# Subtracting the weights' low parts on VectorE instead of GpSimd, in the first group of a hybrid decoder's second stage

## The reference

```python
proj = xn @ w_in
qkv = silu(causal_depthwise_conv(proj[..., :GDN_QKV_W], conv_w))
...
sol = triangular_solve(tmat, rhs)              # within each chunk
v_new = u_c - w_c @ s                          # scan over the chunks, state s
o_c = qd_c @ s + qk_c @ v_new
s = s * dl_c + kd_c^T @ v_new
```

## Time and profile before

| | |
|---|---|
| median of three runs | 2783.84 us (2783.05 to 2786.7) |
| profiled execution, first to last instruction | 2785.0 us |
| PE busy | 2502.1 us (90%) |
| DVE busy | 1675.2 us (60%) |
| ACT busy | 1132.9 us (41%) |
| POOL busy | 457.1 us (16%) |
| POOL `p_wlo` (L1178), 72 instructions | 106.3 us, mean 1486 ns |

### The profile page before, as it was taken

One profiled execution on the slowest core, in us unless ns is written; L12 is line 12 of the kernel. 1 busy time (PEld: TensorE's weight loads), 2 busy tenths in 40 slices (PEclk: granted clock), 3 DMA queues, 4 the chain that ended last, 5 costly groups with the idle time before them and its releaser, 6 DMA issues. The chain is left out here.

```text
span 2785.0 us, 50427 instructions
## 1 busy us (share of the span) xinstructions
PE 2502.1 (90%) x17193; PEld 2202.9 (79%) x17193; DVE 1675.2 (60%) x3904; ACT 1132.9 (41%) x3326; POOL 457.1 (16%) x345
## 2 busy tenths in 40 slices
PE   5468888799999999999999779999997899999997
PEld 4467777789999899999999648878885677777775
DVE  4357676677777777777777322333332566666764
ACT  4244454444444444444444234433332233333332
POOL 0033333310000000000000012200001232233331
PEclk8689999999999999999999689999998899999998
DMA  6664444533445543443443057743456122222221
GB/s 192 196 250 148 138 154 149 188 124 127 157 134 174 161 131 127 145 135 132 138 152 113 21 175 260 253 169 140 170 200 241 65 86 83 71 75 68 85 69 48
DMA packets 273814, 392.79 MB, mean 141 GB/s; under 512 B 79282, under 2 KB 187906, under 8 KB 273442
## 3 DMA queue, kind: packets, MB, share of 16 engines
q1 hardware_dynamic: 240066, 370.05, 39.7%
q10 hardware_dynamic: 33632, 21.26, 2.6%
HBM read 267.92 MB, written 123.31 MB: 140 GB/s over the span
## 5 line engine op out<-in xcount | busy, mean ns | idle before, releaser
L1229 PE MATMUL p_psp<-xg,p_whi 128*128 128x264 f32 x4096 | 848.5, 297 | 27.7 <-POOL p_wlo L1178 17.3
L1229 PEld LDWEIGHTS p_psp<-xg,p_whi 128*128 128x128 f32 x4096 | 661.1, 193 | 32.3 <-issue 23.0
L1229 PE MATMUL p_psp<-xg,p_wlo 128*128 128x264 f32 x2048 | 610.5, 298 | 0.0
L1229 PEld LDWEIGHTS p_psp<-xg,p_wlo 128*128 128x128 f32 x2048 | 395.0, 193 | 0.0
L981 DVE SCALAR_TENSOR_TENSOR p_acc<-p_proj,p_taps,p_acc 128x528 f32<-128x528 f32 x288 | 250.3, 869 | 4.6
L1824 PE MATMUL first_q<-first_w,p_o 128*128 128x512 f32 (+1 forms) x864 | 206.5, 399 | 18.0 <-DVE first_w L1788 18.0
L2366 PE MATMUL first_q<-first_w,p_hT 128*128 128x512 f32 x720 | 195.4, 412 | 13.2 <-DVE p_q L2252 12.9
L1824 PEld LDWEIGHTS first_q<-first_w,p_o 128*128 128x128 f32 (+1 forms) x864 | 157.1, 184 | 60.7 <-issue 15.0
L862 ACT ACTIVATE p_sig<-p_sig 128x528 f32<-128x528 f32 x128 | 82.5, 644 | 289.7 <-DVE p_sig L983 289.6
L2366 PE MATMUL p_pso<-p_wo,p_oT 128*128 128x512 f32 x768 | 192.3, 401 | 7.9 <-DVE p_oT L2278 4.2
L1824 PE MATMUL p_psz<-p_wk,p_o 128*128 128x512 f32 x768 | 181.3, 392 | 0.0
(11 more groups left out here) (263 smaller groups left out, 4665.2 us busy)
## 6 DMA issues: line engine op xcount, KB each, us to landing
p_whi<-w_dram SPq DMA_DIRECT2D x92, 512.0 KB, 4.1
p_wlo<-w_dram SPq DMA_DIRECT2D x92, 512.0 KB, 5.0
raw<-w_a_in SPq DMA_DIRECT2D x36, 512.0 KB, 6.6
w_dram<-p_whi SPq DMA_DIRECT2D x34, 512.0 KB, 4.1
w_dram<-p_wlo SPq DMA_DIRECT2D x34, 512.0 KB, 5.3
p_o<-hT_dram SPq DMA_DIRECT2D x34, 512.0 KB, 4.7
hT_dram<-p_hT SPq DMA_DIRECT2D x32, 512.0 KB, 3.3
p_hT<-hT_dram SPq DMA_DIRECT2D x30, 512.0 KB, 4.0
```

The lines of the kernel that those rows point to most:

```text
L1229: ins = nc.tensor.matmul(ps_p[half_][:, 0:HALF], (w_hi, w_lo)[i][:, f, kc * P:(kc + 1) * P], xg[:, g % 2, j, kc, half_ * HALF:(half_ + 1) ...
```

## The change

`split_low` moves from GpSimd's program to VectorE's, with the same operands, the same wait for ScalarE's high part (`hi_ready`) and the same signal when it is done (`lo_ready`). In a slot it stands behind the taps and ahead of the solve rows. The six calls of the prologue move too: VectorE does them after the constants have arrived and before it waits for the zeroed scratch. Nothing else changes.

```diff
@@ block.vector
+            def split_low(it, f, part):
+
+                cols = slice(part * D // 2, (part + 1) * D // 2)
+                dve.wait_ge(hi_ready, 2 * (NF * it + f) + (part + 1))
+                nc.vector.tensor_tensor(w_lo[:, f, cols], w_raw[:, f % 2, cols], w_hi[:, f, cols].bitcast(f32),
+                                        ALU.subtract).then_inc(lo_ready, 1)
...
                     for item, f, part in slot.taps:
                         convolve(item, f, part)
+                    for item, f, part in slot.split:
+                        split_low(item, f, part)
                     for q, i in slot.rows:
                         solve_row(q, i)
...
             dve.wait_ge(const_in, 16 * N_CONST)
+            for f in range(NF - 1):
+                for part in range(2):
+                    split_low(0, f, part)
             dve.wait_ge(zeroed, 32)
             run(dve, step)
@@ block.gpsimd
-            def split_low(it, f, part):
...
-                    for item, f, part in slot.split:
-                        split_low(item, f, part)
 
             pool.wait_ge(cleared, 1)
-            for f in range(NF - 1):
-                for part in range(2):
-                    split_low(0, f, part)
             run(pool, step)
```

## The result

The kernel after takes 2798.06 us (median of 4 runs, 2794.54 to 2801.13) against 2783.52 before: 1.0055 times [1.0041, 1.0069], slower by 14.5 us. In a second series it took 2797.18 against 2779.40, 1.0063 [1.0049, 1.0077]. The forecast was slower, 2804 us, range 2784 to 2817.

What follows compares the result with a forecast made beforehand. PE waits for VectorE, chiefly for p_r, and VectorE pays for GpSimd's work. Terms -1.2 + 2 - 2 + 18.5 + 3 = +20.3 us on the profiled 2785.0 give 2805, or 2804 us on the median; range 2784 to 2817.

Steps and rivals of the forecast that it cites:

- Price of one: One 128x512 subtraction on VectorE takes 0.62 us of queue time (0.61 to 0.69), in place of 1.5 on GpSimd.
- Slots 5 to 9: Four subtractions and a 0.7 us wait against 3.8 us of relief: -0.3 for each of seven heads, -2 us in all.
- the 0.9 that was to stay: Last 0.9 us of excess in slots 5 to 9; if it stays, that term's upper bound is +3.5 us.
- Slots 14, 15 and 21: Second subtraction delays p_X by 0.55 us; after slot 21's taps the q part's clamp comes at about 383.8 instead of 383.48.
- Slot 23: VectorE waits for ScalarE's copy, then its subtraction stands for GpSimd's SiLU: p_r 2.8 us late, 1.8 without GpSimd.
- six meetings at 2.8, turns of 59 us: Slot 23's delay after heads 1 to 7: 6 x 2.8 + 1.75 = 18.5 us; heads take 55 and 59 us.
- the turns swallow it: Rival: the new wait runs beside some 3.15 us at the loop's turns, three of six meetings cost nothing; 2788 us, 13%.
- the start costs all of it: Rival: head 0's term at 6 us and the clock's at 6; 2814 us and above, 8%.
- relief wins: Rival: VectorE's queue gains more than it gets, slot 23's wait hidden, a head gains about 1 us; 2775 us, 9%.
- Clock: Longer PE idling, 4.7 us instead of 1.9, lowers its granted clock: 0.5 us for each of six, 3 us (0 to 6).
- The start: Two prologue subtractions at 0.62 us instead of at most 1.52 shorten PE's first wait: 1.2 us saved (0.6 to 1.8).
- Head 0: VectorE waits in slots 7 and 14 for load-bound copies; p_nU almost 6 us later, costing 2 us (0 to 6).

Runs made afterwards that it cites:

- e5: The kernel before with 24 tiny memsets at VectorE's start, so its loop begins at instruction 340, nothing else changed: 2768.73 us, 0.9961.
- e10: The kernel before with VectorE only waiting for ScalarE's copy in slot 23, all subtractions on GpSimd, plus 24 memsets (loop at 340): 2784.12 us, 1.0020.
- e4: The kernel after, with GpSimd's SiLU of q held until VectorE's subtraction in slot 23 is done: 2789.71 us, 1.0033.
- e8: The kernel after, with slot 23's subtraction one place later, in the next step behind the first p_r: 2770.39 us, 0.9965.
- e6: The kernel after with 200 tiny memsets in VectorE's idle places at the stage's start, so its loop begins at instruction 540: 2801.62 us, 1.0079.
- e3: The kernel before, all subtractions on GpSimd, VectorE only waiting in slot 23 for ScalarE's copy: 2798.23 us, 1.0056.
- e11: The kernel after with its subtractions spread on VectorE over slots where it idles, plus 6 memsets (loop at 343): 2741.98 us, 0.9862.
- e1: The kernel before with only the prologue's six subtractions moved to VectorE, the loop's still on GpSimd: 2787.08 us, 1.0021.
- e12: Subtractions at the same spread places as e11, but all on GpSimd, the prologue's too, with 24 memsets (loop at 340): 2770.86 us, 0.9963.

## Why the prediction was right, and where it was not

The sum +20.3 us met +14.5 and +17.8, but it is a difference of two numbers of which I had only one. From the medians: moving the code to its new place -10.7 (e5 less before); the wait +15.4 (e10 less e5); the rest of the change, the subtraction behind that wait and its collision above all, +13.1 (after, 2797.2, less e10), of which 7.5 go when POOL gives way (e4). Together +17.8. Without the new place of its code the change thus costs 28.5 us, 8 more than my sum. That the total lay so near is luck: the -10.7 that I hadn't seen made up for terms that I had too small, the clock's above all.

- *Price of one, 0.62 us (0.61 to 0.69).* 0.69 where POOL is away, the upper bound, and a mean of 818 ns.
- *Slots 5 to 9, -2 us in all.* Right in sign. DVE's timeline, kernel after:

```profile
353.17 0.35 DVE L1118 SCALAR_TENSOR_TENSOR p_state<-p_state,p_elast,p_psc 128x128 f32<-128x128 f32 x1 [0.49 <-PE p_psc L1347]
354.24 0.69 DVE L1010 TENSOR_TENSOR p_wlo<-raw,p_whi 128x512 fp32r<-128x512 f32 x1 [0.72 <-ACT p_whi L843]
...
357.64 0.37 DVE L1034 COPY p_Xbt<-p_Xb 40x256 f32<-40x256 f32 x1
...
360.00 1.57 DVE L981 SCALAR_TENSOR_TENSOR p_acc<-p_proj,p_taps,p_acc 128x528 f32<-128x528 f32 x2
```

  The wait of 0.7 us is there (0.72), the copy fell from 0.96 to 0.37, two taps from 2.40 to 1.57. ACT's first sigmoid step stands 10.24 us behind that state update (363.41), before 11.04: -0.8 a head at this point. The ordinary heads of e8, with all but slot 23's subtraction in these places, are 0 to 2 us shorter than e5's, some 0.7 in the mean; head 8 shows 2.6 us, 43.3 against 45.9. The upper bound, +3.5, doesn't follow from the 0.9 that was to stay: 7 x (-0.3 + 0.9) is +4.2.
- *Slots 14, 15 and 21.* PE's wait for `p_X` grew as said (5.3 us in six waits, before 2.4, from 165 to 590 us), but taps of 1.57 in place of 2.47 paid more back: the clamp came 35.0 us behind the state update, before 35.7; I had it 0.3 later, not 0.65 earlier.
- *Slot 23, 2.8 us.* Right to the tenth: wait 1.04, subtraction 1.68, `p_r` 5.34 us behind the clamp in place of 2.59. The Trainium skill's rule (SBUF — State Buffer, section "Who interferes with whom") that the later of two such instructions stands for the other holds here with 0.69 against 1.68 us.
- *The step that failed: six meetings at 2.8, turns of 59 us.* The five ordinary heads grew by 2.4 to 3.6 us, to 53.8 to 55.4, as forecast; the turns stayed at 55.2 and 56.6, since the fetch of some 2.6 us left them. With the fetch put back (e6) they take 59.9 and 58.7, and PE's wait for `p_r` is 42.4 us, close to the 45 that I had named; that forecast was for a kernel whose code lies like the old one's.
- *The rival "the turns swallow it".* Its number for the turns (no loss) came true, its mechanism did not: in e6 4.47 us of idle come behind wait and subtraction, and e3's turn had 3.61 behind its wait. The time at the turn was never spare; it went for another reason.
- *The rival "the start costs all of it".* Its terms give -1.2 + 6 - 2 + 18.5 + 6 = 27.3, so 2811 and not 2814. Neither it nor "relief wins" came true.
- *Clock, +3 us (0 to 6).* Too small. Windows from 165 to 590 us (us, busy PE, PEld, DVE, ACT, POOL, granted clock, DMA share, GB/s) of before, after, e5, e10 and e11:

```profile
165.00:590.00 425.00, 349.68 (x2666) 330.11 (x2667) 297.47 (x764) 205.42 (x644) 146.33 (x121) 0.96 0.47 158
```

```profile
165.00:590.00 425.00, 346.00 (x2550) 325.75 (x2549) 294.34 (x805) 200.26 (x633) 47.74 (x59) 0.92 0.44 149
```

```profile
165.00:590.00 425.00, 352.74 (x2733) 331.56 (x2733) 307.67 (x790) 208.92 (x654) 146.29 (x121) 0.98 0.47 160
```

```profile
165.00:590.00 425.00, 348.22 (x2628) 328.31 (x2628) 294.73 (x756) 200.25 (x634) 143.40 (x119) 0.94 0.45 153
```

```profile
165.00:590.00 425.00, 378.91 (x2973) 356.83 (x2973) 329.90 (x907) 223.92 (x705) 53.01 (x61) 0.98 0.50 167
```

  The granted clock, 1.00 being the upper level of 2.4 GHz, is 0.96, 0.92, 0.98, 0.94 and 0.98, while PE stood 26.1, 35.0, 21.7, 28.9 and 9.6 us for `p_r`. The sum of these waits alone does not set it: e1 has 33.2 us at 0.96, e12 26.7 at 0.98. What does is open. The projection's matmuls, some 1500 in this stretch, took 307 and 303 ns in the mean before (high and low parts), 312 and 308 after, 302 and 299 in e5, 308 and 304 in e10. The high parts in e5, then e10:

```profile
L1231 PE MATMUL p_psp<-xg,p_whi 128*128 128x264 f32 x1064 | 228.0, 302 | 5.6 <-ACT p_proj L854 5.6
```

```profile
L1234 PE MATMUL p_psp<-xg,p_whi 128*128 128x264 f32 x1012 | 223.4, 308 | 5.6 <-ACT p_proj L854 5.6
```

  An estimate from these, with one profiled execution of each kernel: 5 ns x 1500 = 7.5 us from before to after, and (6 x 1000 + 5 x 500) ns = 8.5 us from e5 to e10. With its 7.7 us of late `p_r` that is 16.2 us, against the 15.4 that the wait alone cost: by this estimate the wait on PE's path was paid about twice.
- *The start, -1.2.* From the stage's first memset to the first pair of projection matmuls 129.50 - 120.53 = 8.97 us before, 126.39 - 118.76 = 7.63 after: -1.3. PE after:

```profile
126.39 0.78 PE L1229 MATMUL p_psp<-xg,p_whi 128*128 128x264 f32 x2 [15.94 <-DVE p_wlo L1010]
```

- *Head 0, +2.* It ends 1.6 us later in spite of that start: +2.9. The subtraction ahead of `p_nU` stood 3.44 us for ACT's copy, as said, and `p_nU` came 43.54 us behind the first memset in place of 40.67: 2.9 us later, where I had almost 6. In e6, with the same subtractions, head 0 takes 72.1 us as well.

## What to carry to other kernels

In a queue that runs in order, look less at what moved work costs than at which instruction stands behind it and what the moved one waits for: one subtraction ahead of a state step cost some 27 us, one place later nothing. A wait that keeps TensorE idle can be paid a second time through the granted clock, here by the estimate above. And before a few tenths of a per cent are laid to an edit that adds or removes instructions in or ahead of a loop, compare the instruction queues' packets inside the loop in both traces; a control with a few idle instructions costs little and may itself be the gain.

## What the hardware showed that I had not expected

VectorE fetched its program anew in each pass of a loop of 323 instructions in one place (11 packets of 8 KB from 300 to 540 us; over the kernels with such packets, idle times of 3.3 to 6.9 us at the turns) and not at the turns of a loop of 355 in another (1 packet, ahead of the first turn). The trace names no releaser for such an idle time; the packets of the instruction queue beside it do.
